# Sixteen modulation pieces move from a mixer into the feed-forward behind it, and modulation sums into the norms behind mixers

## What is computed

```python
c_act = jax.nn.silu(c)
for l in range(DEPTH):                                  # two layers
    mod = (c_act @ ada_w[l] + ada_b[l])[:, None, :]     # 1024 x 6144
    sh1, sc1, g1, sh2, sc2, g2 = jnp.split(mod, 6, axis=-1)
    h = _rmsnorm(x, norm_mix_w[l]) * (1 + sc1) + sh1
    x = x + g1 * _mixer(h, ...)                         # attention, mLSTM, w_out
    h = _rmsnorm(x, norm_ffn_w[l]) * (1 + sc2) + sh2
    x = x + g2 * _conv_ffn(h, ...)
return _rmsnorm(x, final_norm_w)

def _conv_ffn(h, w_up, conv_w, conv_b, w_down):
    u = _causal_dwconv(h @ w_up, conv_w, conv_b)        # three taps
    a, val = jnp.split(u, 2, axis=-1)                   # 2816 each
    return (jax.nn.gelu(a) * val) @ w_down
```

## Time and profile before

| | us |
|---|---|
| three runs | 2253.01, 2257.86, 2257.97 |
| median | 2257.86 |
| the profiled execution | 2263.85 |
| its span, first to last instruction | 2262.0 |
| mean granted TensorE clock (share of 2.4 GHz) | 0.97 |

### The profile page before, as it was taken

How to read it: one execution, slowest core, us unless ns; L and a number is a source line. 1 busy time by engine, 2 the same in 40 slices (tenths; PEclk the granted TensorE clock), 3 DMA queues, 4 the chain that set the end, 5 groups by cost and what they waited for, 6 DMA issues and landing times.

```text
span 2262.0 us, 33384 instructions
## 1 busy us (share of the span) xinstructions
PE 2184.0 (97%) x13877; PEld 1960.0 (87%) x13877; DVE 1751.2 (77%) x1892; ACT 1231.6 (54%) x1374; POOL 54.0 (2%) x101
## 2 busy tenths in 40 slices
PE   6999999999999999999999989989999999999998
PEld 5989999987888788788888879868899998888998
DVE  5987777868899898989999847778766665665665
ACT  3724444636777777677777725532455545434554
POOL 1000000000000000000000000000000000000000
PEclk8999999989999999999999979989999999999999
DMA  9886985647999999999999936847465455344552
GB/s 318 299 307 252 332 311 169 231 149 280 379 379 352 369 375 368 366 372 380 356 374 375 360 101 171 298 152 266 168 198 169 131 130 154 94 149 148 188 175 87
DMA packets 339039, 578.55 MB, mean 256 GB/s; under 512 B 48098, under 2 KB 208954, under 8 KB 326594
## 3 DMA queue, kind: packets, MB, share of 16 engines
q1 hardware_dynamic: 324604, 475.34, 61.7%
q0 software_dynamic: 13824, 100.67, 11.5%
q10 hardware_dynamic: 454, 0.34, 0.1%
HBM read 575.26 MB, written 1.05 MB: 255 GB/s over the span
## 4 chain that ended last, share of the span: by engine, by line
PE 83%; DVE 8%; ACT 4%; DMA 3%; issue 2%; DVEq 0%; ACTq 0%; POOL 0%; POOLq 0%
PE bank L580 82%; ACT arena L1542 2%; DMA ada_in<-in_ada_w 2%; DVE w_low L2090 2%; DVE ada_acc L2098 1%; DVE arena L2098 1%; PE bank L1294 1%; DVE arena L2090 1%; DMA ring<-in_moe_w 1%; DMA ring<-in_w_out 1%; DVE arena L2567 1%; ACT mix_hi L1542 1%; ACT L1542 1%; DVE arena L2543 0%; DVE x L2098 0%
## 5 line engine op out<-in xcount | busy, mean ns | idle before, releaser
L2090 DVE TENSOR_TENSOR w_low<-ring,moe_w_hi 128x2048 fp32r<-128x2048 f32 x264 | 594.5, 2285 | 10.3 <-ACT moe_w_hi L1542 8.9
L1542 ACT ACTIVATE moe_w_hi<-ring 128x2048 fp32r<-128x2048 f32 x264 | 506.3, 1918 | 167.2 <-DMA ring<-in_moe_w 128.2
L580 PE MATMUL bank<-h_hi,w_hi 128*128 128x256 f32 x1056 | 262.3, 287 | 5.0 <-DVE w_low L2090 4.1
L580 PE MATMUL bank<-h_hi,w_low 128*128 128x256 f32 x1056 | 260.0, 283 | 0.0
L580 PE MATMUL bank<-mix_h_hi,mix_hi 128*128 128x256 f32 x800 | 238.1, 299 | 10.6 <-ACTq L1539 6.0
L580 PE MATMUL bank<-mix_h_hi,w_low 128*128 128x256 f32 (+2 forms) x848 | 245.7, 291 | 0.0
L580 PE MATMUL bank<-h_low,mix_hi 128*128 128x256 f32 x800 | 214.8, 284 | 0.0
L2098 DVE SCALAR_TENSOR_TENSOR ada_acc<-ada_in,c_col,ada_acc 128x2048 f32<-128x2048 f32 x84 | 197.1, 2347 | 20.3 <-DMA ada_in<-in_ada_w 15.9
L1542 ACT ACTIVATE arena<-bank 128x512 f32<-128x512 f32 (+2 forms) x172 | 90.5, 526 | 213.9 <-PE bank L580 210.5
L580 PEld LDWEIGHTS bank<-h_hi,w_hi 128*128 128x128 f32 x1056 | 200.5, 190 | 7.4 <-DVE w_low L2090 4.5
L580 PEld LDWEIGHTS bank<-h_hi,w_low 128*128 128x128 f32 x1056 | 201.9, 191 | 0.4 <-issue 0.3
(11 more groups left out here) (214 smaller groups left out, 4653.1 us busy)
## 6 DMA issues: line engine op xcount, KB each, us to landing
ring<-in_moe_w SPq DMA_DIRECT2D x264, 1024.0 KB, 6.6
ada_in<-in_ada_w POOLq DMA_DIRECT2D x96, 1024.0 KB, 7.5
ring<-in_w_in SPq DMA_DIRECT2D x56, 1024.0 KB, 5.5
ring<-in_ffn_w_up SPq DMA_DIRECT2D x44, 1024.0 KB, 7.7
ring<-in_ffn_w SPq DMA_DIRECT2D x33, 1024.0 KB, 7.8
ring<-in_ffn_w_down SPq DMA_DIRECT2D x22, 1024.0 KB, 4.9
ring<-in_w_out SPq DMA_DIRECT2D x16, 1024.0 KB, 5.5
ring<-in_w_br_mla SPq DMA_DIRECT2D x4, 1024.0 KB, 5.1
```

Of the source, the lines that this page charges most:

```text
L580: ins = nc.tensor.matmul(out, lhsT, rhs, start=start, stop=stop, skip_group_check=shared)
L1542: return nc.scalar.activation(out, in_, f, **kw)
L2090: return nc.vector.tensor_tensor(out, a, b, op)
```

## The change

- Layer 3's pieces: the first eight stay in `mixer2(0)`, three right at its start behind VectorE's `modulation(2, 16, 32)`, one ahead of the copy of `ckv`, four where four were, before the attention's steps. The sixteen others go into conv0, behind `split_down` of the odd blocks: two each at f = 1 to 11, one each at f = 13 to 19. `ada_finish(3)` goes behind conv0's last block.
- Modulation sums of columns 32 to 47, for both layers of the second block: 32 to 39 on TensorE between the output product and `norm_sum` (bank 6), on VectorE behind `residual`; 40 to 47 behind `norm_sum` (bank 2), on VectorE behind the eight multiplies of the norm and before `h_low`. Two fillers follow instead of four. They are no longer made ahead of mixer 0 nor in mixer 1's attention.

```diff
+MIXER_PIECES = range(3 * ADA_PER_LAYER, 3 * ADA_PER_LAYER + KB)
@@ TensorE
+            def conv_ffn_norm():
+                fill(6)
+                modulation(6, 4 * KB, 5 * KB)
+                norm_sum()
+                fill(2)
+                modulation(2, 5 * KB, MODS)
+                keep_busy(2)
@@ TensorE, mixer2, attention steps
-                        if li:
-                            if step == 0:
-                                fill(5)
-                            modulation(5, 4 * KB + 2 * step, 4 * KB + 2 * step + 2)
@@ TensorE, the order of stages
             keep_busy(1, 3)
-            modulation(7, 4 * KB, 5 * KB)
-            keep_busy(1, 3)
-            modulation(7, 5 * KB, MODS)
             mixer2(0)
-            norm_sum()
-            keep_busy(4)
+            conv_ffn_norm()
             ffn("u", 0, F0["conv0"], start_modulation)
...
             mixer2(1)
-            norm_sum()
-            keep_busy(4)
+            conv_ffn_norm()
             ffn("u", 1, F0["conv1"])
@@ VectorE, mixer2
-                modulation(2 + li, 2 * KB, 4 * KB if li else MODS, 7)
-                pieces = iter(range(3 * ADA_PER_LAYER, 4 * ADA_PER_LAYER) if li == 0 else ())
+                modulation(2 + li, 2 * KB, 4 * KB, 7)
+                pieces = iter(MIXER_PIECES if li == 0 else ())
...
+                ada_next(3)
...
+                    if key[0] == "ckv":
+                        ada_next(1)
...
-                    if step < 6:
-                        ada_next(1)
-                if li:
-                    modulation(3, 4 * KB, MODS, 5)
...
-                residual((0, 5, 3, 7), 16, "wout_psum", lambda j: ada_next((2, 2, 2, 1)[j]))
-                if li == 0:
-                    ada_finish(3)
+                residual((0, 5, 3, 7), 16, "wout_psum")
+                modulation(2 + li, 4 * KB, 5 * KB, 6)
@@ VectorE, conv_ffn
+                pieces = iter(range(MIXER_PIECES.stop, 4 * ADA_PER_LAYER) if li == 0 else ())
...
                     if f % 2 == 0:
                         split_low("u", li, f // 2 + 1)
+                    else:
+                        for n in itertools.islice(pieces, 2 if f < 12 else 1):
+                            ada_piece(n)
                 if li == 0:
+                    ada_finish(3)
                     low(("kr", 1, 0))
@@ VectorE, the order of stages
             mixer2(0)
             norm(scale_a[:, 1, :], h, "norm_mul")
+            modulation(2, 5 * KB, MODS, 2)
             split_h(5, h_hi, 24)
...
             mixer2(1)
             norm(scale_a[:, 1, :], h, "norm_mul")
+            modulation(3, 5 * KB, MODS, 2)
             split_h(7, h_hi, 24)
```

## The result

The changed kernel takes 2280.64 us (median of five runs, 2273.30 to 2285.99) beside 2257.97 us for the kernel before: a ratio of 1.0092, 95% interval 1.0073 to 1.0111. A second set gave 2280.93 beside 2260.08 us, 1.0077 (1.0060 to 1.0095). So the change costs 17.4 to 20.8 us by the ratios; the forecast was +11.8 and 2269.7 us, with a range that ended at 2277. The direction was right and the size too small: by 5.6 to 9 us by the ratios, by 10.9 us by the median.

What follows compares the result with a forecast made beforehand. TensorE bounds conv0 and VectorE the later part of mixer 0; with the pieces, VectorE's chain would set conv0's pace. Terms: -12.9 - 1.9 + 3.6 + 6.0 + 15.0 + 2.0 = +11.8, from 2257.86 to 2269.7 us; range 2258 to 2277.

Steps and rivals of the forecast that it cites:

- the term for the end of conv0: Last down block of conv0: TensorE first waits 2.0 us for VectorE's ada_finish(3); +2.0 us, bounds 1.5 and 3.
- the +1.0 for the pieces ahead of mixer 0's attention: Mixer 0: the four pieces before the scores can no longer all be preloaded, about 1.0 us more.
- the -1.9 for the sums taken out of it: Attention of mixer 1, also used for mixer 0's pace: column sums exposed every second step, 1.9 us gained without them.
- Conv0's loop, +15.0: VectorE's in-order steps: 19.9 us per two-piece pair, 17.5 with one, against TensorE's 17.2; +15.0 us, bounds 13 and 16.
- Early pieces at nothing: Start of mixer 0: three pieces fill VectorE's wait for ScalarE, the fourth its wait for TensorE; cost 0.
- The start of the feed-forwards, +3.0 each: First up matmul waits for VectorE's add to free bank 2: +3.0 us, twice, together +6.0, bounds 2.2 and 7.6.
- Mixer 0, -12.9: Mixer 0 without sixteen pieces needs 169.8 us, not 182.69: a gain of 12.9 us, bounds 10 and 15.
- The rival of the mixers' extra gain: The mixers gain 5 us more and conv0 is at its lower bound, -2: 2262.5 us; 8%.
- the chances behind "same": Whole kernel between 2251.1 and 2264.6 us: half the conv0 rival, the mixers' extra gain, a third of the clock rival; 18%.
- Conv0 hides the pieces: Rival: conv0 stays at 17.2 us per pair, so the +15.0 is gone: -3.2, 2254.7 us; 7%.
- The clock stays up at both starts: Rival at both feed-forward starts: 2 x 1.1 in place of 6.0 us, in all +8.0, 2265.9 us; 15%.
- The mixer gives back only half: Rival in mixer 0: early loads hold up first projections, the VectorE-ScalarE chain binds attention; +6, 2276 us; 12%.

Runs made afterwards that it cites:

- the even blocks: Changed kernel with one piece at each even block of conv0, the other five at odd blocks 3, 7, 11, 15 and 17: 2269.58 us, 1.0042 of before.
- The early release: Changed kernel with ada_finish(3) one block earlier in conv0, behind block 20 and not 21: 2278.83 us, 1.0065 of before.
- the wide products: Changed kernel with ada_finish(3) behind block 20, plus four 384-column fillers among layer 3's sums at conv0's end: 2277.19 us, 1.0070 of before.
- the early addition: Changed kernel with VectorE's addition of the last sums ahead of the norm's eight multiplies, for both layers: 2277.13 us, 1.0071 of before.
- the pieces alone at even blocks: Kernel before with only the sixteen pieces moved, mostly to even blocks, and ada_finish(3) behind block 20: 2258.33 us, 0.9986; again 2258.00 us, 0.9985.
- the first experiment: Kernel before with only the sixteen pieces moved into conv0, all modulation sums left where they stood: 2268.82 us, 1.0034 of before.
- layer 3's sums alone: Kernel before with only layer 3's sums moved, from mixer 1's attention into the norm behind it and behind its reciprocal: 2266.01 us, 1.0025 of before.
- the first set's four: Four kernels of one set of runs, among them the one that moved only the sixteen pieces, 2268.82 us, 1.0034 of before.

## Why the prediction missed, point by point

The mechanism that carried most of the forecast, VectorE's chain in conv0, was right. The step that failed is the term for the end of conv0, "+2.0, bounds 1.5 and 3": it measured +5.1, because the wait was priced without the half clock behind it. Two smaller terms failed as well, the +1.0 for the pieces ahead of mixer 0's attention and the -1.9 for the sums taken out of it. These three, 3.1, 1.9 and 1.1 us, are about what separates the forecast's +11.8 from the traces' +17.7; what the medians have above the traces, up to 5 us, stays open.

- **Conv0's loop, +15.0: right.** +15.5 measured; the pair takes 19.88 us where the sum of VectorE's own steps gave 19.9, and TensorE waits. That 60 us of idle time did not help is shown by the even blocks, which take 9.3 us off by order alone.
- **Early pieces at nothing: right, as far as the spread tells.** Copy to preceding reciprocal 79.06 us, 78.99 before; over all traces 77.7 to 79.1 with the early pieces and 76.6 to 79.0 in the three without.
- **The start of the feed-forwards, +3.0 each: right in kind, and a mixture of two prices.** The wait for bank 2 came as written. It costs 1.4 us where the clock stays (nine starts in seven traces), 2.6 to 2.8 where it is at 0.50 for some 3 us (conv0 in three traces), 4.0 where it is there for some 6 us (conv1 in two, with 1.5 more in the loop behind). My bounds, 1.1 and 3.8, were those two ends. In the changed kernel's own traces the starts gave 2.6 and 1.4, 2 us less than I counted for both.
- **The end of conv0, +2.0: too small, by 3.1 us.** This is the failing step. The wait itself was 1.50 us. What I did not price is the sums behind it at half clock, 6.38 us and not 3.6, and the down product of block 21 at half clock too. The early release took 3.6 of the 5.1 us back, and the wide products showed the clock to be the sums' doing. How early it falls differs: five traces with the late release have 7.5 to 8.1 us here, and a sixth, where it fell some 2 us later, 5.9, the upper bound of the forecast.
- **The sums taken out of attention, -1.9 in each mixer: too large, by 1.2 to 1.3 us.** In seven of the nine traces with layer 3's sums in the norm, mixer 1 is 1.1 to 1.2 us longer from its copy to norm 1; with 1.8 for the sums ahead of `norm_sum`, only 0.6 to 0.7 came back. The attention does end 1.4 us sooner (its last reciprocal 62.3 us behind the copy, 63.7 before), but the next step then waits for TensorE. Before and after, VectorE at that step, and a window of TensorE alone that holds the fall of its clock there:

```profile
1945.87 0.17 DVE L2488 RECIPROCAL small<-small 128x2 f32<-128x2 f32 x1 [0.58 <-ACTq L1537]
1948.08 0.74 DVE L2095 TENSOR_SCALAR arena<-bank,small 128x256 f32<-128x256 f32 x2 [0.83 <-PE bank L580]
...
1949.00:1953.00 4.00, 3.77 (x24) 0.57 0.00 0
```

```profile
1956.60 0.17 DVE L2491 RECIPROCAL small<-small 128x2 f32<-128x2 f32 x1 [0.58 <-ACTq L1537]
1959.46 0.74 DVE L2095 TENSOR_SCALAR arena<-bank,small 128x256 f32<-128x256 f32 x2 [2.11 <-PE bank L581]
...
1957.00:1965.00 8.00, 7.44 (x36) 0.57 0.15 52
```

  TensorE stands still for 2.69 us ahead of this step, where before it had two shorter waits (1.80 and 0.83), and its clock falls some 4 us sooner behind the copy and is low for twice as long. So the sums' going gained 1.4 us, and the longer fall took some 0.7 of it back. Three more traces agree. They lack another fall of the clock, at the copy itself, which the others have. Two of them, with the sums in the norm (the even blocks, the early addition), have the short fall and take 169.6 us; the third, with the sums in the attention (the pieces alone at even blocks, first trace), has the long one and takes 170.0: 0.4 more, close to 1.4 and 0.7 less the 1.8.
- **Mixer 0, -12.9: too large, by 1.9 us.** 171.7 and 171.5 us measured without the sums in its norm (173.8 in a third trace, with the longer fall of the clock), 169.8 forecast. The 169.8 was mixer 1's 170.65 less 1.9 for the sums and 1.0 more for the pieces ahead of the attention. With 0.7 for the sums and the 1.7 that the pieces cost there in the first experiment it is 170.65 - 0.7 + 1.7 = 171.7. That the 1.7 us are the pieces' is read from one mixer beside the other; no kernel without them was run.
- **The median.** The terms as traced give +17.7, the two sets 17.4 and 20.8 by the ratios and 21 to 23 by the medians. The rest may be what the starts do in other executions, as layer 3's sums alone cost 5.6 us and have the 4.0 us start in their trace; no trace of the changed kernel shows it.
- **The range.** Its upper end, 2277, is +19. The bounds of the terms add up to +20.2, and to +23.2 with the +3 that the prediction itself names for the loads; the +17.4 and +20.8 lie inside that. The rival of the mixers' extra gain sums to 2262.7, not 2262.5, and the chances behind "same" to 16 or 17%, not 18%; neither matters.
- **The rivals.** "Conv0 hides the pieces" is out. "The clock stays up at both starts" was half so in the trace and untrue in the mean of the runs. "The mixer gives back only half" named a loss of 6 where it was 2.3, and no trace shows the early loads holding anything up.

## What to carry to other kernels

Where an in-order engine trades data with another one in every step, its idle share is no room: write down its steps for one turn of the loop, and put new work only where the sum leaves a wait, such as the 1.38 us ahead of a split here. When an instruction that covered a wait is itself made to wait, price it again at the lower clock, with what stands behind it. And a saving on a path of two engines is worth the slack of the second one: look at which wait grows next.

## What the runs showed of the chip

- TensorE's granted clock fell from 1.00 to 0.50 behind or among 32 one-column passes although the engine was busy without a gap (seven traces, such as before the change and with the early release), and stayed at 1.00 when a product of 384 columns stood ahead of every eight of them (one trace). The Trainium skill (TensorE: Matmul & The Clock Gate, Part 1) ties the gate to how busy TensorE has been; in the profile's busy time these windows are all 1.00, so that column can't show what the gate reacts to.
- The same 2.88 us wait in the same place left the clock at 1.00 in some executions and cost 2.7 us more at 0.50 in others. A wait of 2.69 us in mixer 1's attention was followed by some 7 us at 0.50, where two waits of 1.80 and 0.83 us with 1.6 us of work between them were followed by some 3.5. In conv0's loop, with VectorE as the bound, a fall of the clock cost little: the pair from 1648.41 to 1668.30, with a granted clock of 0.76 from 1655 to 1660, took 19.89 us like its neighbours, and a pair with one piece and 0.57 from 1732 to 1736 took 18.11 beside 17.43.
- Leaving the change aside, executions of one kernel differ by 8 to 17 us in the sets of nine runs and more, along with their mean granted clock: over the runs of six kernels (before, after and the first set's four), 0.001 of it goes with about 1.5 us.
